# Output projection of four layers: rows gated two blocks ahead, its elementwise work spread over three engines

## The reference

```python
y_l = jnp.concatenate([yr_l * jax.nn.silu(rg_l), ya_l * jax.nn.silu(ag_l),
                       yn_l * jax.nn.silu(ng_l)], axis=-1) @ w_out
x = _layer_norm(DEEPNORM_ALPHA * x + gate[:, None] * y_l, ln_g, ln_b)
```

```python
y = jnp.einsum('bsc,cd->bsd', mixed * jax.nn.silu(gate), w_out[l])
h_res = _layer_norm_2(DEEPNORM_ALPHA_2 * h_res + y, ln_g[l], ln_b[l])
```

## Time and profile before

| | us |
|---|---|
| median of 3 runs | 5117.96 |
| lowest and highest | 5108.36 and 5126.37 |
| the profiled execution | 5092.85 |
| its span in the profile | 5091.1 |
| PE busy in the span | 4344.3 (85%) |
| DVE busy | 2557.3 (50%) |
| ACT busy | 1460.7 (29%) |
| POOL busy | 1123.7 (22%) |

### The profile page before, as it was taken

One profiled execution on the slowest core, in us unless ns is written; L12 is line 12 of the kernel. 1 busy time (PEld: TensorE's weight loads), 2 busy tenths in 40 slices (PEclk: granted clock), 3 DMA queues, 4 the chain that ended last, 5 costly groups with the idle time before them and its releaser, 6 DMA issues. The chain is left out here.

```text
span 5091.1 us, 102962 instructions
## 1 busy us (share of the span) xinstructions
PE 4344.3 (85%) x43250; PEld 3319.0 (65%) x43250; DVE 2557.3 (50%) x4264; ACT 1460.7 (29%) x2611; POOL 1123.7 (22%) x834
## 2 busy tenths in 40 slices
PE   5899888968988699989985998599688879968898
PEld 3778688855657577678883666487444568844356
DVE  3465444456657447544445666400565660045666
ACT  1133222224540123222223551100344410024441
POOL 2233133301012223233321011322021122210201
PEclk7999899999999799999998999799899999989999
DMA  5655522342234556633313134332311443341124
GB/s 200 197 183 191 161 72 59 78 185 53 61 114 143 172 168 211 197 101 75 78 35 118 50 82 159 136 99 93 109 36 42 129 142 96 95 126 48 27 58 169
DMA packets 536799, 579.24 MB, mean 114 GB/s; under 512 B 140724, under 2 KB 440244, under 8 KB 533220
## 3 DMA queue, kind: packets, MB, share of 16 engines
q1 hardware_dynamic: 408740, 493.80, 30.9%
q10 hardware_dynamic: 127616, 78.95, 5.3%
HBM read 374.66 MB, written 202.19 MB: 113 GB/s over the span
## 5 line engine op out<-in xcount | busy, mean ns | idle before, releaser
L1118 PE MATMUL pr_acc<-hH,pr_wh 128*128 128x512 f32 (+1 forms) x2184 | 831.4, 381 | 46.5 <-issue 46.5
L1119 PE MATMUL pr_acc<-hL,pr_wh 128*128 128x512 f32 (+1 forms) x2184 | 812.3, 372 | 0.0
L1120 PE MATMUL pr_acc<-hH,pr_wl 128*128 128x512 f32 (+1 forms) x2184 | 812.0, 372 | 0.0
L1118 PEld LDWEIGHTS pr_acc<-hH,pr_wh 128*128 128x128 f32 x2184 | 414.8, 190 | 142.0 <-issue 69.1
L1162 POOL TENSOR_TENSOR pr_wl<-pr_w,pr_wh 128x1024 fp32r<-128x1024 f32 x118 | 282.8, 2397 | 995.9 <-DVE pr_wh L1182 995.9
L1119 PEld LDWEIGHTS pr_acc<-hL,pr_wh 128*128 128x128 f32 x2184 | 414.7, 190 | 74.1 <-issue 1.0
L1120 PEld LDWEIGHTS pr_acc<-hH,pr_wl 128*128 128x128 f32 x2184 | 413.3, 189 | 74.3
L2176 ACT ACTIVATE an_p<-an_p,an_stat 128x1280 f32<-128x1280 f32 (+5 forms) x372 | 339.5, 913 | 276.6 <-DVE an_stat L2252 272.9
L1182 DVE CAST pr_wh<-pr_w 128x1024 fp32r<-128x1024 f32 x118 | 82.4, 698 | 620.8 <-PE pr_acc L1120 601.0
L2248 DVE CUSTOM_DVE_ANT_0 an_p<-an_s,an_mask 128x256 f32<-128x256 f32 (+8 forms) x308 | 274.8, 892 | 175.7 <-PE an_s L2119 79.5
L1152 ACT COPY pr_out<-pr_acc 128x1024 f32<-128x1024 f32 (+2 forms) x118 | 123.8, 1050 | 833.6 <-PE pr_acc L1120 833.6
(11 more groups left out here) (313 smaller groups left out, 8328.2 us busy)
## 6 DMA issues: line engine op xcount, KB each, us to landing
pr_w<-in_w_in ACTq DMA_DIRECT2D x108, 512.0 KB, 4.1
CHK<-ri_out SPq DMA_DIRECT2D x24, 1920.0 KB, 8.0
rk_in<-CHK SPq DMA_DIRECT2D x120, 384.0 KB, 5.5
UT<-pr_out SPq DMA_DIRECT2D x45, 640.0 KB, 4.4
U<-pr_out SPq DMA_DIRECT2D x50, 512.0 KB, 4.3
mod_w<-in_w_mod SPq DMA_DIRECT2D x16, 1536.0 KB, 13.2
mo_w<-in_w_out SPq DMA_DIRECT2D x16, 1024.0 KB, 10.3
BIAS<-wb_bias SPq DMA_DIRECT2D x8, 1600.0 KB, 7.0
```

Source lines behind the costliest of these rows:

```text
L1118: nc.tensor.matmul(out, wh[:, u, k, 0:m], hi, start=(k == 0), stop=False)
L1119: nc.tensor.matmul(out, wh[:, u, k, 0:m], lo, start=False, stop=False)
L1120: ins = nc.tensor.matmul(out, wl[:, u, k, 0:m], hi, start=False, stop=(k == KT - 1))
```

## The change

ScalarE takes two pieces of work: `upper(t)` rounds the gated rows into `mo_yh`, and `norm(t)` normalises (scale and bias in one activation). GpSimd makes the bias (`power` has a second instruction) and adds `ln_b` in `shift(t)`; only the last block's add stays on VectorE. `normed(t)` on VectorE is cut in two, `summed(t)` up to the statistics and `scaled(t)`, the multiplication by `ln_g`, and the gating of block t + 2 stands between them. `mo_z` has three buffers, `mo_small` two. A store of block t - 1 follows `norm(t)` on ACT. The transfer of the ready groups has a semaphore of its own and is issued ahead of `x`. In the first product `turn(1)` comes two column groups earlier.

```diff
-                        if k == NK - 3:
-                            turn(1, 1)
+                        if k == NK - 5:
+                            turn(1)
```

```diff
@@ scalar
+                def upper(t):
+                    u = t % 2
+                    act.wait_ge(yt.sem, yt.nth(t + 1))
+                    if ncm:
+                        act.wait_ge(yg_in.on(u), yg_in.step(t, u))
+                    if t >= 2:
+                        act.wait_ge(mm.sem, mm.nth(t - 1))
+                    nc.scalar.copy(YH[:, u], YT[:, u]).then_inc(y_hi.sem, 1)
+
+                def norm(t):
+                    act.wait_ge(nb.sem, nb.nth(t + 1))
+                    zz, small = z[:, t % NZ, :], sm[:, t % 2, :]
+                    nc.scalar.activation(zz, zz, ACT.Identity, bias=small[:, 15:16], scale=small[:, 14:15]).then_inc(nrm.sem, 1)
...
                 for t in range(nblk):
-                    if t + 1 < nblk:
-                        tanh(t + 1, (t + 1) % 2)
-                    store(t, t % 2)
+                    if t + 2 < nblk:
+                        tanh(t + 2)
+                        upper(t + 2)
+                    norm(t)
+                    if t:
+                        store(t - 1)
+                store(nblk - 1)
@@ gpsimd
+                    pool.wait_ge(pw.sem, pw.nth(t + 1))
+                    nc.gpsimd.tensor_tensor(small[:, 15:16], small[:, 12:13], small[:, 14:15], ALU.mult).then_inc(nb.sem, 1)
+
+                def shift(t):
+                    pool.wait_ge(sc.sem, sc.nth(t + 1))
+                    zz = z[:, t % NZ, :]
+                    nc.gpsimd.tensor_tensor(zz, zz, vecs[:, 1, :], ALU.add).then_inc(fin.sem, 1)
...
                 for t in range(nblk):
+                    power(t)
+                    if t + 2 < nblk:
+                        lower(t + 2)
                     if t + 1 < nblk:
-                        tails(t + 1, (t + 1) % 2)
-                    power(t, t % 2)
+                        shift(t)
@@ vector
+                def scaled(t):
+                    dve.wait_ge(nrm.sem, nrm.nth(t + 1))
+                    zz = z[:, t % NZ, :]
+                    V.tensor_tensor(zz, zz, vecs[:, 0, :], ALU.mult).then_inc(sc.sem, 1)
+                    if t + 1 == nblk:
+                        dve.wait_ge(sc.sem, sc.nth(t + 1))
+                        V.tensor_tensor(zz, zz, vecs[:, 1, :], ALU.add).then_inc(fin.sem, 1)
...
+                gated(1)
                 dve.wait_ge(cst.sem, cst.after(1))
                 for t in range(nblk):
-                    if t + 1 < nblk:
-                        gated(t + 1, (t + 1) % 2)
-                    normed(t, t % 2)
+                    summed(t)
+                    if t + 2 < nblk:
+                        gated(t + 2)
+                    scaled(t)
```

More of the change, by code:

```diff
@@ L2331, in mixed_out @@
         vecs = core.sb(s, "mo_vecs", [P, len(vectors), DM])
[L2332 to L2333 removed]
+        z = core.sb(s, "mo_z", [P, NZ, DM])
+        sm = core.sb(s, "mo_small", [P, 2, 16])
         ps = core.ps(s, "mo_ps", 8)
@@ L2358, in _ @@
                 weights(0)
-                load(0, 0)
+                load(0)
                 for k in range(1, NK // 2):
                     weights(k)
-                load(1, 1)
+                load(1)
                 for i, v in enumerate(vectors):
@@ L2384, in _ @@
                 weights(0)
-                tanh(0, 0)
+                tanh(0)
+                upper(0)
                 for k in range(1, NK // 2):
                     weights(k)
+                tanh(1)
+                upper(1)
                 for t in range(nblk):
-                    if t + 1 < nblk:
-                        tanh(t + 1, (t + 1) % 2)
-                    store(t, t % 2)
-                for u in range(2):
-                    act.wait_ge(stored.on(u), stored.total(nblk, u))
+                    if t + 2 < nblk:
+                        tanh(t + 2)
+                        upper(t + 2)
+                    norm(t)
+                    if t:
+                        store(t - 1)
@@ L2395, in _, with lower, power @@
+                store(nblk - 1)
+                for u in range(NZ):
+                    act.wait_ge(stored[u].sem, stored[u].after((nblk + NZ - 1 - u) // NZ))
             @block.gpsimd
             def _(pool):
-                def tails(t, u):
+                def lower(t):
+                    u = t % 2
                     pool.wait_ge(y_hi.sem, y_hi.nth(t + 1))
                     nc.gpsimd.tensor_tensor(YL[:, u], YT[:, u], YH[:, u], ALU.subtract).then_inc(y_lo.sem, 1)
-                def power(t, u):
+                def power(t):
+                    small = sm[:, t % 2, :]
@@ L2451, in _, with gated @@
                     if t + 1 < nblk:
-                        turn(t + 1, (t + 1) % 2)
-                    product(t, t % 2)
+                        turn(t + 1)
+                    product(t)
             @block.vector
             def _(dve):
-                for sig in (yt, z_ok, fin):
-                    sig.open(dve)
-                def gated(t, u):
+                def gated(t):
+                    u = t % 2
                     dve.wait_ge(y_in.on(u), y_in.step(t, u))
```

126 lines of the change are left out of this document (61 added, 65 removed).

## The result

| | kernel before | changed kernel |
|---|---|---|
| runs side by side on one chip | 5122.16 us median of 4 (5108.36 to 5133.18) | 5061.09 us median of 4 (5046.59 to 5067.65) |
| profiled execution, own time | 5092.85 us | 5067.65 us |
| its span | 5091.1 us | 5065.9 us |
| DVE busy | 2557.3 us | 2505.9 us |
| ACT, POOL busy | 1460.7, 1123.7 us | 1536.7, 1221.7 us |

The ratio is 0.9896, 95% interval 0.9868 to 0.9924: faster by 1.0%, 61 us between the medians (39 to 68 by the interval). The prediction said 41 us off and 5077.0, range 5048 to 5102.

What follows compares the result with a forecast made beforehand. Bound: latency from queue order, PE waiting for POOL's `mo_yl`. 47.6 gained less 2.0 ports, 1.4 starts, 3.2 tails gives 41.0 us, off the median 5117.96: 5077.0 us, 8 in 10 range 5048 to 5102.

Steps and rivals of the forecast that it cites:

- the ring: Chain from one product's end through VectorE, tanh, gating and `mo_yl` to product t + 2: 14.6 us, PE waits the rest.
- waits 39.8 and 30 x 0.26: In the product loops: PE's waits on `mo_yl` all go, with 0.26 us beside each of 30, 47.6 us gained.
- slower restart of 0.09: PE's product after a wait: about 0.09 us longer, part of the 0.26 a wait costs beside its length.
- The ports: DVE and POOL exclude each other in gated rounds, so PE waits before the last products of two calls: +2.0 us.
- only near a call's end: Gated calls: DVE falls back 0.45 us a block, so `mo_yl`'s slack of 1.25 us is eaten only there.
- The starts: Start of each of four calls: `upper(0)` takes 1.01 us for the cast's 0.70, plus its semaphore; 1.4 us in all.
- The tails: After each call's last statistics: small operations, second POOL operation, ACT's norm and a handover, 0.8 us a call, 3.2 in all.
- the ports bite harder: Rival: POOL's power gets in before the gating, gated round 12.3 us; gain 24 to 36, time 5082 to 5094, chance 0.19.
- a power well above 0.56: Sign of being wrong: POOL's power taking well above its 0.56 us.
- The tables: Rival on ScalarE: Identity and tanh share no table, two 1.28 us loads a round; gain about 34, time 5084, chance 0.05.
- The gain does not appear: Rival: PE's waits return as transfer waits or a lower clock; within 15 us of now, 5103 to 5133, chance 0.10.
- slower: Rival: gating and second sum operation each wait out a POOL operation, gated round 15.6 us; +38, 5156, chance 0.06.

Runs made afterwards that it cites:

- e1: The changed kernel once more with no edit, beside the kernel before: median 5047.51 us, ratio 0.9885.
- e5: The kernel before with no edit, profiled once more: 5117.24 us in one execution, its four calls 563.4 us.
- e6: The kernel before with no edit, profiled yet again: 5117.87 us in one execution, its four calls 564.5 us.
- e10: The kernel before with the gated product written back to PSUM, so the sum's second operation has one SBUF input: 5108.83 us, ratio 1.0006.

## Why the prediction was right

**The mechanism** was right: the bound was the latency of the ring, and its 39.8 us of waits went. Between the two first profiles the four product loops (from the end of the first product) became 16.8, 12.4, 8.8 and 9.0 us shorter, 47.0 in all; the step "waits 39.8 and 30 x 0.26", 47.6, was right to 0.6 us. The 0.26 was put together wrongly, though. A product takes 10.97 to 11.02 us up to the next turn with a wait before it or without, so there is no slower restart of 0.09; an ungated turn costs 0.79 us without a wait (11.77 less 10.98) and not 0.87, and the two errors cancel.

**The ports** were forecast at +2.0 and cost 0 in PE's time. The hold of the sum's second operation was sized well: 1.0 us assumed, 1.16 measured at its full size (2.39 against 1.23). Two other steps were off. The round from sum to the end of `scaled` was priced at 10.85 without the hold and took 10.5 (1560.54 to 1571.06). And the hold doesn't come at once: it grows by 0.11 to 0.16 us a round from 0.48, so the round stays inside PE's 11.48 up to block 6 and reaches 11.60 at block 7 (1629.32 to 1640.92), where 11.9 was forecast. DVE falls back only in the last rounds of the 10-block call, as "only near a call's end" has it, and by so little that 0.7 us of the slack are left.

**The starts** were forecast at +1.4. To the first product they took 2.2 us more and in it 0.6, 2.8 together. `upper` and its handover were right: from the gating of block 0 to the first product each call takes 0.35 us more, 5.23 for 4.88 gated and 6.04 for 5.69 ungated, 1.4 in all. `turn(1)` had its rows, and PE doesn't wait for it in any of the four calls. The other 1.4 us lie ahead of that gating and in the first product, and such stretches differ as much between executions of one kernel: to the gating the four calls take 37.9, 38.0 and 38.3 us together in three executions of the kernel before, 38.7 and 37.4 in two of the changed one; in the first product 56.9, 56.3 and 55.5, and 57.5 and 56.1. So nothing ties them to the change. **The tails** were forecast at +3.2 and cost +2.2, 0.55 each: the bias product took 0.20 us, bounds 0.10 and 0.56, and the overlap of the small operations was better than reckoned. `norm` took 1.24 for 1.15. In sum -47.0 + 2.2 + 0.6 + 2.2 = -42.0 against -41.0. That the sum is right to 1 us is in part luck: the gain of the loops was put 0.6 us too high and the cost of the starts 1.4 too low, the ports 2.0 and the tails 1.0 too high.

**The rivals.** Of "the ports bite harder" the measurement shows another order: the gating issues first and takes its undisturbed 0.81 to 0.82, and it is the power that is held, 1.06 us for 0.55 in the gated rounds and up to 1.46 in the ungated ones. The prediction had named a power well above 0.56 as a sign of being wrong; the sign came, and cost nothing, since `norm` stands behind `upper` on ACT: the bias product ends at 1589.65, and `upper` runs from 1589.87 to 1590.92. The tables fell: the only two loads are those of the tanh line, as before. "The gain does not appear" and "slower" fell with the waits. The slower case needed a POOL operation at both points of DVE; at the gating there was none.

**What the range held and I didn't know.** 5077 came from taking the 41 us off the median of 5117.96. The medians differ by 61 (here) and 59 (e1), and I had noted only that its profile lay 25 us under its median, "the calls are the same work in either". That sentence is the step that failed. The same work took 554.4 us in the profiled execution and 563.4 and 564.5 in two others, since PE's clock falls behind the longer waits of the slow rhythm. The change takes away the waits and with them the falls of the clock, about 9 us more than the rows I had could show. 42 + 9 = 51; the remaining 8 to 10 us are in the steps outside the calls, which scatter between 4523 and 4554 over all executions here (4547 on average in three of the kernel before, 4546 in the two of the changed one), so no run ties them to the change. They stay open, and may be no more than the scatter of the medians: by their intervals the two differences are 39 to 68 and 48 to 69 us, and 51 lies in both.

## What to carry to other kernels

When one engine waits a little in every round, look for the one order of the queues that takes the next round's input off the last round's finish, before moving work between engines: here the order alone was worth 57 us and the division of the work, 27 us by itself, nothing clear on top. A round that is a little longer than that of the engine that sets the period costs nothing while the call is short enough for the slack to last: look at the last blocks of a call and not at one in the middle. Price a wait of TensorE at two rates, its own length and the slow microseconds behind it, and profile the kernel before more than once if its profile doesn't lie at its median. Where the waits can't be removed, a few matmuls into an unused part of PSUM are a cheap trial.

## What the runs showed of the hardware that was not expected

- The clock fell to its lower level behind 11 of the 13 waits of 2.37 to 2.43 us in the first call of the kernel before and of e5, e6 and e10, and behind none of 1.44 to 1.48 us. From its start to the next turn the product behind it took 12.4 to 12.6 us instead of 11.0, twice 13.9.
- DVE and POOL hold each other in both directions, and small operations too: POOL's 128x1 power 1.06 us for 0.55 behind DVE's gating; `mo_yl` 2.90 for 2.35 behind a tensor_scalar with one SBUF tile of 128x1024, and then DVE's two-input multiplication 3.30 for 1.23 behind that `mo_yl`. The Trainium skill, SBUF — State Buffer, section "Who interferes with whom", names both kinds of DVE instruction, those with two SBUF inputs and `tensor_scalar`: whoever issues first gets the shared pair for the whole instruction. The durations here agree: the held one ended 0.09 to 0.16 us earlier than if it had only begun when the other ended.
- GpSimd's 128x1 multiplication takes 0.20 us where its power of that size takes 0.55: the size is not the cost, the function is.
